# Attention scores of two head groups issued in pairs on 64-row tiles, in a two-layer hybrid decoder trunk

## What is computed

```
D_MODEL, SEQ, DEPTH, HEAD_DIM = 1024, 256, 2, 64
NSA_HEADS, NSA_KV_HEADS, NSA_GROUP = 8, 2, 4

def masked_softmax(s, mask):
    s = jnp.where(mask, s.astype(jnp.float32), NEG_INF)
    p = jax.nn.softmax(s, axis=-1)
    return jnp.where(mask, p, 0.0)

    s = jnp.einsum('bgqhd,bgqnd->bgqhn', qb, kg) * scale        # selection branch
    p = masked_softmax(s, mask[:, :, :, None, :])
    ...
    s_w = jnp.einsum('bnqghd,bnkgd->bnghqk', qb, kwin) * scale  # window branch
    p_w = masked_softmax(s_w, wmask[None, :, None, None])
    ...
    g = jax.nn.sigmoid(gate_logits.astype(jnp.float32)).reshape(B, T, G, HPG, N_BRANCH)
    o = g[..., 0:1] * o_cmp + g[..., 1:2] * o_sel + g[..., 2:3] * o_win

def token_mixer(h, w_in, ...):
    proj = h @ w_in
    ...
    return jnp.concatenate([o_a, o_b, o_c], axis=-1) @ w_out
```

## Time and profile before

| | |
|---|---|
| median of 3 runs | 1275.2 us |
| profiled execution: its time, its span | 1274.92 us, 1272.9 us |
| TensorE busy | 98% of the span |
| VectorE, ScalarE busy | 78%, 67% |
| attention part of layer 0 (score 0 to the last xT) | 76.1 to 158.0 us |
| the same of layer 1, from score 0 | from 411.6 us |
| granted TensorE clock, mean | 0.997 |

### The profile page before, as it was taken

The page is one execution under the profiler, slowest core; times in us unless marked ns, Lnnn a source line. Parts: engine busy times, 40 slices in busy tenths (PEclk is TensorE's granted clock), DMA queues, the critical chain, the costliest instruction groups (busy, mean ns, idle before and its releaser), DMA issues.

```text
span 1272.9 us, 16264 instructions
## 1 busy us (share of the span) xinstructions
PE 1253.7 (98%) x6313; PEld 1015.9 (80%) x6313; DVE 996.8 (78%) x1110; ACT 856.6 (67%) x1225; POOL 31.0 (2%) x21
## 2 busy tenths in 40 slices
PE   9999999999999999999999999999999999999996
PEld 8797588888779866788888888888888888888885
DVE  4886455455569646998999989889889889889997
ACT  4335264444451544978878888878878878878885
POOL 0000000000000000010000000000000000000300
PEclk9999999999999999999999999999999999999999
DMA  9433194442521336899999999999999999999991
GB/s 370 165 143 133 71 388 175 174 184 103 198 100 71 143 132 267 340 401 372 394 369 372 390 380 374 386 371 383 389 369 381 389 372 358 396 373 351 415 370 39
DMA packets 38625, 367.62 MB, mean 289 GB/s; under 512 B 4112, under 2 KB 7312, under 8 KB 11152
## 3 DMA queue, kind: packets, MB, share of 16 engines
q1 hardware_dynamic: 35808, 356.56, 71.2%
q0 software_dynamic: 1440, 5.24, 1.1%
q10 hardware_dynamic: 1296, 4.72, 0.9%
HBM read 360.73 MB, written 5.77 MB: 288 GB/s over the span
## 4 chain that ended last, share of the span: by engine, by line
PE 92%; DVE 4%; ACT 2%; issue 0%; DMA 0%; DVEq 0%; ACTq 0%
PE ps L661 88%; PE ps L664 4%; ACT arena L1294 1%; DVE blocks L1674 1%; DVE wlU L1856 1%; DVE arena L1692 0%; DVE wlD L1863 0%; ACT arena L1304 0%; DMA x<-x_in 0%; ACT xn L1196 0%; ACT L1286 0%; ACT L1341 0%; DVE arena L1765 0%; DVE xn L1596 0%; DVE ringl L1635 0%
## 5 line engine op out<-in xcount | busy, mean ns | idle before, releaser
L1856 DVE TENSOR_TENSOR wlU<-ring,whU 128x2048 fp32r<-128x2048 f32 x196 | 448.8, 2290 | 57.6 <-ACT whU L1386 53.1
L1386 ACT ACTIVATE whU<-ring 128x1024 fp32r<-128x1024 f32 x396 | 417.6, 1060 | 60.8 <-PE ps L661 53.2
L661 PE MATMUL ps<-whU,hTh 128*128 128x512 f32 x880 | 352.7, 401 | 0.8 <-DVE wlU L1856 0.8
L661 PE MATMUL ps<-whU,hTl 128*128 128x512 f32 x880 | 345.0, 392 | 0.0
L661 PE MATMUL ps<-wlU,hTh 128*128 128x512 f32 x880 | 343.0, 390 | 0.0
L1863 DVE TENSOR_TENSOR wlD<-ring,whD 128x2048 fp32r<-128x2048 f32 x97 | 222.1, 2290 | 39.2 <-ACT whD L1398 39.0
L1398 ACT ACTIVATE whD<-ring 128x1024 fp32r<-128x1024 f32 x194 | 205.2, 1066 | 58.9 <-PE ps L661 52.7
L661 PEld LDWEIGHTS ps<-whU,hTl 128*128 128x128 f32 x880 | 165.1, 188 | 36.1
L661 PEld LDWEIGHTS ps<-wlU,hTh 128*128 128x128 f32 x880 | 166.0, 189 | 32.4
L661 PEld LDWEIGHTS ps<-whU,hTh 128*128 128x128 f32 x880 | 165.3, 188 | 32.7 <-DVE wlU L1856 1.0
L661 PE MATMUL ps<-whD,gTh 128*128 128x512 f32 x428 | 168.6, 394 | 0.5 <-DVE gTl L1881 0.5
(11 more groups left out here) (232 smaller groups left out, 1224.7 us busy)
## 6 DMA issues: line engine op xcount, KB each, us to landing
ring<-moe_in SPq DMA_DIRECT2D x88, 2048.0 KB, 8.4
ring<-moe_in SPq DMA_DIRECT2D x88, 1024.0 KB, 8.6
ring<-ffn_in SPq DMA_DIRECT2D x11, 2048.0 KB, 7.6
ring<-mix_in SPq DMA_DIRECT2D x5, 3072.0 KB, 10.8
ring<-ffn_in SPq DMA_DIRECT2D x11, 1024.0 KB, 6.9
ring<-mix_in SPq DMA_DIRECT2D x4, 2048.0 KB, 10.5
ring<-mix_in SPq DMA_DIRECT2D x2, 2176.0 KB, 8.6
ring<-mix_in SPq DMA_DIRECT2D x2, 2112.0 KB, 8.1
```

The lines of the kernel that those rows point to most:

```text
L661: return nc.tensor.matmul(o, lhsT, rhs, start=first, stop=last, skip_group_check=True)
L1386: A(whU[:, p, :], ring[:, f.slot(J), p * PIECE:(p + 1) * PIECE], ACT.Copy).then_inc(s_hi, 1)
L1856: V.tensor_tensor(wlU[:, w, :], raw, whU[:, w, :].bitcast(F32), ALU.subtract).then_inc(s_lo, 1)
```

## The change

Neighbouring units are now the two head groups of the same branch, tile and heads: units 0, 1, 6 and 7 are narrow and the others wide, where 0, 3, 6 and 9 were narrow. At an even unit TensorE issues the scores of units k and k+1 together: both causal matmuls, and then for each head a 64-row matmul of group 0 and one of group 1, on partitions 0 to 63 and 64 to 127, into two banks. At an odd score TensorE does nothing. `kT` has one key head per half and no zeros; `apart` keeps the addresses behind it as they were. ScalarE copies the keys in one instruction instead of two, and GpSimd's zeroing and its semaphore are gone. rets 1, convT, cnorm 0 and hid 1 change their places in `BESIDE`. The banks are handed out by another rule: a bank that holds scores is skipped until its unit's probT, banks 4 to 7 stay in the rotation until their own output starts, and units 10 and 11 take theirs from banks 0 to 3.

```diff
--- before.py
+++ after.py
@@ -68,7 +68,7 @@
 
-UNITS = [(br, g, i, c, n) for br in range(2) for g in range(2) for i, c, n in ((0, 0, 4), (1, 0, 2), (1, 2, 2))]
+UNITS = [(br, g, i, c, n) for br in range(2) for i, c, n in ((0, 0, 4), (1, 0, 2), (1, 2, 2)) for g in range(2)]
 
@@ -90,8 +90,8 @@
 
-BESIDE = {0: [("rets", 0)], 1: [("rets", 1)], 2: [("convT", 0)],
-          3: [("reto", 0), ("hid", 0), ("cnorm", 0)], 4: [("croot", 0), ("hid", 1), ("retnorm", 0)], 5: [("cnorm", 1)],
+BESIDE = {0: [("rets", 0), ("rets", 1)], 1: [("convT", 0)], 2: [("cnorm", 0)], 3: [("reto", 0), ("hid", 0)],
+          4: [("croot", 0), ("retnorm", 0)], 5: [("hid", 1), ("cnorm", 1)],
           6: [("retnorm", 1)], 7: [("cmpkv", 0), ("conv_pw", 0)],
@@ -134,17 +133,35 @@
 _used = [0] * BANKS
+
+
+def take(key, b):
+    _used[b] += 1
+    GROUP[key] = (b, _used[b])
+
+
 for _l in range(DEPTH):
-    _n = 2
+    _n, _held = 2, set()
     for _at, (_stage, _k) in enumerate(MIXER[_l]):
+        _open = set(range(BANKS)) - {OUT_BANK[_r] for _r in range(4) if MIXER[_l].index(("out", _r)) < _at}
+        if _stage == "probT":
+            _held.discard(GROUP[(_l, "score", _k, 0)][0])
+        if _stage == "score":
+            for _u in (_k, _k + 1) * (_k % 2 == 0):
+                while _n % BANKS in _held or _n % BANKS not in (_open if _k < len(UNITS) - 2 else range(OUT_BANK[0])):
+                    _n += 1
+                take((_l, "score", _u, 0), _n % BANKS)
+                _held.add(_n % BANKS)
+                _n += 1
+            continue
         for _j in range(STATED.get((_stage, _k), PSUM_GROUPS.get(_stage, 0))):
             if (_stage, _k) in FIXED:
-                _b = FIXED[_stage, _k]
-            else:
-                _b = _n % (BANKS if _at < NARROW[_l] else OUT_BANK[0])
+                take((_l, _stage, _k, _j), FIXED[_stage, _k])
+                continue
+            while _n % BANKS in _held or _n % BANKS not in _open:
                 _n += 1
-            _used[_b] += 1
-            GROUP[(_l, _stage, _k, _j)] = (_b, _used[_b])
+            take((_l, _stage, _k, _j), _n % BANKS)
+            _n += 1
 
@@ -303,7 +320,8 @@
         qT = early("qT", [P, HPG, T])
-        kT = early("kT", [P, 2, 2, T])
+        kT = early("kT", [P, 2, T])
+        early("apart", [P, 2, T])
         sig = early("sig", [P, NC, T])
...
@@ -794,23 +811,27 @@
                         is_full(token_major(begin(l, stage, k), l, RET, 768, k, 256, 512), l, stage, k)
+                    elif stage == "score" and k % 2:
+                        continue
                     elif stage == "score":
                         keys = (i + 1) * P
-                        o = begin(l, stage, k)
+                        o = [begin(l, stage, k + u) for u in range(2)]
                         if k == 0:
                             freed(pe, l, "ks")
-                            pe.wait_ge(s_kzero, 2 * (l + 1))
                             freed(pe, l, "q", 0)
                             pe.wait_ge(s_fold, 1)
-
-                        ov = o[:, 0:n * keys].rearrange("p (n k) -> p n k", n=n)
-                        mm(ov[:, :, i * P:keys], identb[:], spread(causalb[:], 1, n), True, False)
+                        for u in range(2):
+                            ov = o[u][:, 0:n * keys].rearrange("p (n k) -> p n k", n=n)
+                            mm(ov[:, :, i * P:keys], identb[:], spread(causalb[:], 1, n), True, False)
                         for c in range(n):
-                            last = mm(o[:, c * keys:(c + 1) * keys], qT[:, c0 + c, i * P:(i + 1) * P],
-                                      kT[:, g, br, 0:keys], False, c == n - 1)
-                        is_full(last, l, stage, k)
+                            for u in range(2):
+                                z = slice(u * HD, (u + 1) * HD)
+                                last = mm(o[u][:, c * keys:(c + 1) * keys], qT[z, c0 + c, i * P:(i + 1) * P],
+                                          kT[z, br, 0:keys], False, c == n - 1)
+                                if c == n - 1:
+                                    is_full(last, l, stage, k + u)
                     elif stage == "probT":
@@ -1253,10 +1274,7 @@
                         full(act, l, stage)
-                        for g in range(2):
-                            z = slice(g * HD, (g + 1) * HD)
-                            last = A(kT[z, g, :, :], bank(l, stage)[z, :].rearrange("p (c t) -> p c t", c=2), ACT.Copy)
-                        is_free(last, l, stage)
+                        is_free(A(kT[:], bank(l, stage).rearrange("p (c t) -> p c t", c=2), ACT.Copy), l, stage)
                     elif stage == "reto":
@@ -1803,11 +1821,11 @@
                         freed(dve, l, "cpv", k)
-                        for u in (1, 2, 4, 5) if k else (0, 3):
+                        for u in (2, 3, 4, 5) if k else (0, 1):
                             freed(dve, l, "pv", u)
                     elif stage == "osum":
-                        for u in (7, 8, 10, 11) if k else (6, 9):
+                        for u in (8, 9, 10, 11) if k else (6, 7):
                             freed(dve, l, "pv", u)
@@ -2136,13 +2154,6 @@
             pool.wait_ge(s_zero, 2)
-            for l in range(DEPTH):
-                if l:
-                    pool.wait_ge(s_ysum, 2 * NT)
-                for g in range(2):
-                    G.memset(kT[(1 - g) * HD:(2 - g) * HD, g, :, :], 0.0).then_inc(s_kzero, 1)
-                    pool.wait_ge(s_kzero, 2 * l + g + 1)
-
             def fetch(out_rows, sheet, places, done):
```

More of the change, by code:

```diff
@@ L116 @@
 FIXED.update({("xT", 0): 2, ("xT", 1): 3, ("xT", 2): 2, ("xT", 3): 3})
-NARROW = [MIXER[l].index(("out", 0)) for l in range(DEPTH)]
 BANKS = 8
@@ L450, in hybrid_trunk_kernel @@
         s_zero = sem("s_zero")
-        s_kzero = sem("s_kzero")
         s_hTh = sem("s_hTh")
```

## The result

The changed kernel takes 1286.92 us (median of four runs, 1285.61 to 1288.87), the kernel before 1275.38 us on the same chip: a ratio of 1.0086, 95% interval 1.0074 to 1.0098. That is 11.5 us slower, where I had forecast 4.0 us and a range up to 1282.0 us. The profiled execution took 1285.61 us with a span of 1283.7 us, 10.8 us more than the 1272.9 us of before. TensorE's mean granted clock was 0.989 of full speed, before 0.997. This is the fastest of the four executions; the other three took 1.3 to 3.3 us longer at 0.984 to 0.988 and have no trace, so what follows divides 10.8 us and not 11.5.

What follows compares the result with a forecast made beforehand. TensorE, busy 98% of the span, bounds the kernel, rivalled in attention by a ScalarE and VectorE chain. Per layer +2.74 - 0.98 + 0.26 = +2.02 us, +4.0 us on 1275.2 us: 1279.2 us, range 1275.0 to 1282.0 us.

Steps and rivals of the forecast that it cites:

- TensorE's own time: Score matmuls: pairs save 5.25 us per layer; three more mode switches of 0.3 us leave 4.35 us per layer.
- First step: Up to probT 4: pv 2 starts at 90.57 us, probT 4 at 97.45 us, TensorE leading by 1.3 us.
- Second step: Up to the copy of probT 6: it starts at 107.03 us, 0.07 us before its old time; lead used up.
- Third step: At score 10: new 1.8 us wait for bank 0, filled by probT 8; output 0 starts 2.74 us late.
- Sum per layer: Output 0 late +2.74, score 11 gone -0.98, output 1's wait +0.26: +2.02 us; both layers +4.0 us.
- slower still: Rival: tiles don't overlap when both accumulate on the causal tile; +1.76 us more per layer, 1282.7 us; chance 0.09.
- faster: Rival: the wait for bank 0 doesn't bind; 1266.5 us with all leads kept, 1270.9 us with half; chance 0.15.
- no change: Rival: chain over ScalarE and VectorE runs 0.75 us or more earlier per layer; sum below +2.5 us, 1277 us; chance 0.18.

Runs made afterwards that it cites:

- e4: Changed kernel, same order and banks, but scores over all 128 rows against keys held with zeros: 1283.93 us, ratio 1.0062.
- e2: Changed kernel with throwaway matmuls ahead of five of TensorE's waits, in the bank the stage owns: 1281.95 us, ratio 1.0054.
- e7: Changed kernel's paired scores with another order of the stages beside them and banks by longest unused: 1267.03 us, ratio 0.9931.
- e1: Changed kernel with other banks for twenty stages, from the compressed key stage to output 1: 1276.17 us, ratio 1.0017.
- e6: Kernel before, full-height scores, with score 10 taking the bank that probT 8 has just filled: 1289.63 us, ratio 1.0105.
- e9: Kernel of e6 with 18 throwaway matmuls into a free bank ahead of the wait before score 10: 1281.08 us, ratio 1.0036.
- e3: Changed kernel with e1's banks and e2's throwaway matmuls, without those before score 10: 1273.95 us, ratio 0.9986.
- e8: Kernel of e7 with full-height scores and zeroed keys instead of the tiles: 1271.6 us, ratio 0.9967.
- e10: Changed kernel with the BESIDE table of the kernel before; pairs, unit order and rotation rule stay: 1276.38 us, ratio 1.0002.
- e12: Kernel of e7 with four throwaway matmuls before and four after the compressed scores: 1268.67 us, ratio 0.9935.
- e5: Kernel before, same order and banks, with 64-row scores one unit at a time and keys without zeros: 1278.92 us, ratio 1.0023.
- e11: Paired scores in a second order, both hidden stages beside pv 5, conv_pw and cmpkv products one unit earlier than e7: 1266.06 us, ratio 0.9917.

## Why the prediction missed

*TensorE's own time*: right for a pair, 1.63 us for the pair 0/1 as summed from the earlier trace rows. The worth of the tiles per layer, 4.35 us in the text, was not measured in the changed kernel's order; at full clock they are worth 1.25 us there, up to output 0 (e4 against e2), and 2.3 us in e7's order with its six more tiled stretches.

*First step*: right. pv 2 started at 90.74 us (forecast 90.57) and probT 4 at 97.62 (97.45); 0.13 us of each is that score 0 itself came later.

*Second step*: right. Maximum 6 at 99.78 us (99.59), the copy of hid 1 right ahead of the copy of probT 6, and that at 107.18 us (107.03). The lead was used up, and convB waited 1.04 us instead of 0.53.

*Third step*: right in mechanism and size. Where the clock was up until then, in layer 1, score 10 started 41.93 us after score 0, forecast 41.97, behind a wait of 1.62 us for ScalarE's copy of probT 8 (1.8); output 0 waited 0.69 us for the compressed scores (0.76). At full clock (e2) this makes +1.84 us per layer where the sum says +2.02. Undoing the bank choice alone takes it away (e1). The Trainium skill's warning named in the prediction (TensorEngine Tiling (Array Packing), PSUM Pressure) is that row tiles write to different banks; here that means that a pair needs two free banks at once. The effect of 4 us that I forecast is there: 3.7 us of the 10.8.

*The step that failed* is the last line of the third: "Sum per layer: +2.74 - 0.98 + 0.26 = +2.02 us; both layers +4.0 us." It keeps every duration of the old trace, and so the clock at which they were taken. The text named the fall once, as a sentence in the rival "slower still" ("The granted clock falling in the 1.7 us wait would work the same way"), gave it no price and shared a chance of 0.09 with the tiles. In the runs it was worth 5.3 us in the mixers, 2.33 and 2.99 (e2 against the changed kernel). Another 1.65 us come behind them, where the routing's half-clock stretch is 6.8 us long instead of 3.4. That a single wait of 2 us can bring the clock down was shown in the kernel before itself (e6), and that in this place it is the standing and not the scores, the banks or the order, by e9.

The 1.65 us of the routing go with that stretch, not with the stops in the mixers. The part behind the mixers is 1.5 to 2.0 us longer than in the kernel before in all nine traces that have 6.8 us there (the changed kernel, e2, e3, e4, e6, e8, e9, e10, e12), though e2, e3 and e9 have no half-clock stretch in the mixers, and 0.3 to 0.7 us longer in the four that have 3.4 us (e1, e5, e7, e11). Why the stretch is longer in some executions stays open. It need not be the change: fifteen executions of the kernel before lie between 1275.2 us at a mean clock of 0.997 and 1277.8 us at 0.995.

The price could have been had from the old trace. Its routing window from 497 to 501 us has a clock of 0.57, so in this program the clock does fall and stays down for some 3.4 us. A stretch at half clock costs up to half its length where matmuls bind. One such stretch per layer is 1.7 us: +3.4 us on the sum, 1282.6 us. That is still short of the measured time, as the stretches in the mixers were 10 and 7 us long, but it would have moved the range. I also took each wait by itself. From pv 5 to score 10 TensorE stands five times, 4.5 us in layer 1 (0.58 + 0.78 + 0.45 + 1.10 + 1.62), against 1.0 us in the kernel before; the forecast counted only what moved the end.

The rivals: *faster* and *no change* fell, since the bank wait was there in full. *Slower still* by tiles that don't overlap fell with the pair's 1.63 us.

What stays open: the exact condition of the fall. The same kernel e1 kept its clock in five executions of ten; e4 stood 1.62 us before score 10 in both layers and lost the clock in one; e7, e11 and e12 lost it in layer 0, e5 in layer 1 and e8 in both, without a stop right ahead. So standing is a cause, shown by e9, but not the only one. Full-height scores fill some of the waits, and e4's mean clock (0.994 to 0.996) is above the changed kernel's (0.984 to 0.989), so I can't say that the tiles play no part; e6 and e8 say that they are not needed, and e2 that they are not enough.

## What to carry to other kernels

When a change takes work off an engine that then waits, look first at what it waits for: here banks, handed out by a rotation that nobody had aimed, cost 2.8 us per layer (e2 against e1), and another order and other banks turned a kernel with the same 64-row pairs from 11.5 us slower into 9 to 11 us faster, of which order and banks by themselves give 4.6 us (e8). Price each new stop of TensorE twice, by its length and by the stretch at 1.2 GHz that may follow, which in these traces was 3.4 to 10 us long and could cost more than the stop. If a wait can't be removed, fill it with throwaway matmuls in a bank that is free: it took 9.1 of e6's 13.5 us away (e9).

## What the runs showed that I had not expected

A wait of 2.02 us was followed by some 10 us at half clock (e6, layer 0), although TensorE was busy without a gap from its end on. The same program on the same chip had the clock fall or not from one execution to the next, with 1273.3 and 1284.7 us as the ends (e1). The clock also fell, for 3.4 us, behind 29 us in which TensorE never stood (e7, layer 0, from 113.4 us on, after matmuls of 16 to 256 columns), and not in layer 1 of the same execution; with full-height scores (e8) it did so in both layers. The start of score 0 moved between 76.07 and 77.23 us from kernel to kernel, with the same instructions ahead of it, which is 1.1 us that no edit here explains.
